# A table of steps ahead of which TensorE makes products of constants, and modulation rows one in each state step

## The reference

```python
def reference(x, ...):
    x = first_block(...)    # layer 0: gated linear attention (2 x 4 heads, chunks of 64) beside differential attention
                            # layer 1: state-space mixer (SSD, 32 heads in 4 groups, chunks of 128)
                            # each followed by layer norm, SwiGLU (hidden 2816), layer norm
    return second_block(...)  # SwiGLU; window attention beside a gated linear recurrence (HGRN); merge; SwiGLU

def first_block(...):         # per layer
    mod_x = silu(c) @ mod_w[layer] + mod_b[layer]          # modulation: six vectors of 1024
    mod_c = silu(c_ctx) @ mod_w[layer] + mod_b[layer]

def second_block(...):
    mod = silu(c) @ w_ada[l] + b_ada[l]                     # nine vectors of 1024
```

## Time and profile before

| | |
|---|---|
| median of 3 runs | 4111.59 us (4111.22 to 4112.58) |
| profiled execution | 4128.64 us |
| its span, first to last instruction | 4126.8 us |
| mean granted TensorE clock | 0.951 of 2.4 GHz |
| PE busy | 3827.0 us (93%) |
| DVE, ACT, POOL busy | 1596.6, 1431.0, 1181.7 us |

### The profile page before, as it was taken

The page is one execution under the profiler, slowest core; times in us unless marked ns, Lnnn a source line. Parts: engine busy times, 40 slices in busy tenths (PEclk is TensorE's granted clock), DMA queues, the critical chain, the costliest instruction groups (busy, mean ns, idle before and its releaser), DMA issues.

```text
span 4126.8 us, 52620 instructions
## 1 busy us (share of the span) xinstructions
PE 3827.0 (93%) x22147; PEld 3212.8 (78%) x22147; DVE 1596.6 (39%) x2686; ACT 1431.0 (35%) x2313; POOL 1181.7 (29%) x745
## 2 busy tenths in 40 slices
PE   7999889999998999998999899999988879898999
PEld 5877667888877888786888788888777766687888
DVE  4355563111136655655212321111457644332113
ACT  4223344211125434424422332211354536443223
POOL 2011022111132524516222421121433423243224
PEclk9999999999999999998999989999988989899999
DMA  5221133332241111023333412222322211142333
GB/s 177 72 78 42 47 113 108 97 97 91 93 141 37 42 52 50 28 65 125 98 103 105 139 58 67 62 62 64 115 71 62 57 43 32 43 146 82 97 97 108
DMA packets 471974, 336.67 MB, mean 82 GB/s; under 512 B 17609, under 2 KB 445627, under 8 KB 471739
## 3 DMA queue, kind: packets, MB, share of 16 engines
q1 hardware_dynamic: 471056, 333.05, 26.6%
q10 hardware_dynamic: 683, 0.26, 0.0%
HBM read 331.17 MB, written 2.10 MB: 81 GB/s over the span
## 4 chain that ended last, share of the span: by engine, by line
PE 81%; DVE 7%; ACT 4%; POOL 3%; DMA 2%; issue 2%; SPq 0%; ACTq 0%; POOLq 0%; DVEq 0%
PE PS L107 79%; PE PS L115 2%; DVE A L124 1%; POOL RWr L124 1%; DMA MW<-in_mod_w 1%; ACT A L118 1%; ACT L118 1%; POOL TM L124 1%; ACT RWH L121 1%; DVE A L132 1%; POOL A L124 1%; DMA MW<-in_w_ada 1%; DVE SM L144 1%; DVE XT L124 0%; DVE G L124 0%
## 5 line engine op out<-in xcount | busy, mean ns | idle before, releaser
L124 POOL TENSOR_TENSOR RWr<-RW,RWH 128x1024 fp32r<-128x1024 f32 (+2 forms) x316 | 727.9, 2306 | 2326.5 <-ACT RWH L121 2317.8
L107 PE MATMUL PS<-HTH,RWH 128*128 128x512 f32 (+1 forms) x3360 | 1211.1, 360 | 29.5 <-POOL RWr L124 9.2
L107 PE MATMUL PS<-HTr,RWH 128*128 128x512 f32 (+1 forms) x3360 | 1184.7, 353 | 0.0
L107 PE MATMUL PS<-HTH,RWr 128*128 128x512 f32 (+1 forms) x3360 | 1184.1, 352 | 0.0
L107 PE MATMUL PS<-Ar,RWH 128*128 128x512 f32 (+1 forms) x3264 | 825.6, 344 | 13.6 <-DVE XT L132 5.1
L107 PEld LDWEIGHTS PS<-HTH,RWH 128*128 128x128 f32 x3360 | 647.6, 193 | 146.3 <-issue 46.4
L107 PEld LDWEIGHTS PS<-HTH,RWr 128*128 128x128 f32 x3360 | 646.3, 192 | 85.6 <-issue 0.4
L107 PEld LDWEIGHTS PS<-HTr,RWH 128*128 128x128 f32 x3360 | 647.4, 193 | 82.0 <-issue 2.7
L107 PEld LDWEIGHTS PS<-Ar,RWH 128*128 128x128 f32 x3264 | 568.3, 193 | 102.5 <-issue 16.0
L121 ACT ACTIVATE RWH<-RW 128x1024 fp32r<-128x1024 f32 (+2 forms) x474 | 475.0, 1007 | 317.5 <-DMA RW<-in_ffn_w_out 163.6
L107 PE MATMUL PS<-Ar,RWr 128*128 128x512 f32 (+1 forms) x1632 | 555.5, 340 | 0.0
(11 more groups left out here) (193 smaller groups left out, 3790.7 us busy)
## 6 DMA issues: line engine op xcount, KB each, us to landing
RW<-in_ffn_w_in SPq DMA_DIRECT2D x176, 512.0 KB, 3.8
MW<-in_mod_w SPq DMA_DIRECT2D x83, 512.0 KB, 4.7
MW<-in_w_ada SPq DMA_DIRECT2D x72, 512.0 KB, 4.4
RW<-in_ffn_w_out SPq DMA_DIRECT2D x64, 512.0 KB, 3.9
RW<-in_ffn_w_out SPq DMA_DIRECT2D x64, 384.0 KB, 3.3
RW<-in_mix_w_in SPq DMA_DIRECT2D x41, 512.0 KB, 3.8
RW<-in_ssd_w_in SPq DMA_DIRECT2D x40, 512.0 KB, 3.9
RW<-in_ev_w_in SPq DMA_DIRECT2D x24, 512.0 KB, 3.9
```

The lines of the kernel that those rows point to most:

```text
L107: return self._ins(self.real and self.real.matmul(o, l, r, start=start, stop=stop, skip_group_check=True))
L124: return self._ins(self.real and self.real.tensor_tensor(out=o, in0=i0, in1=i1, op=op))
```

## The change

Two things. First, a table `warm` in `plan` names 71 steps by stage and arguments, each with a number from 2 to 11, 268 in sum. Ahead of such a step `tensor_program` calls `turn_over`, which asks `Banks.idle` for a PSUM bank that is free at that step, waits for that bank's last reader, and makes that many f32 products of `k.ident` with the first two matrices of `k.CC`, 256 columns, into it. Nobody reads them, and they signal nothing. If no bank is free nothing is made. Second, `Gla.states` puts `mod` after every state and not only the odd ones, and the two calls pass one row in place of two.

```diff
@@ class Banks
+    def idle(self, p, *key):
+
+        if p.real is None and key not in self.at:
+            at = [b for b in range(8) if 0 > self.back[b] or self.back[b] < self.step]
+            if not at:
+                return None
+            b = min(at, key=lambda b: self.back[b])
+            self.at[key], self.before[key] = (b, 1), [self.holder[b]] if self.holder[b] else []
+        if key not in self.at:
+            return None
+        for held in self.before[key]:
+            if p.real is not None:
+                for event in self.freed[held]:
+                    p.wait_ge(*event)
+        return self.of(*key)
+
...
+def turn_over(p, k, i):
+
+    pv = k.banks.idle(p, "warm", i)
+    if pv is not None:
+        for _ in range(k.warm[i]):
+            p.mm(pv[:, 0:256], k.ident, k.CC[:, 0:2, :].rearrange("p a b -> p (a b)"), True, True)
...
@@ class Gla
     def states(self, mod):
         out = []
         for x in range(11):
-            out += self.one(f"state {x}") + (mod if x % 2 else [])
+            out += self.one(f"state {x}") + mod
         return out
...
@@ def plan
-    order += gla[0].states([("mod", 24)] * 2) + spliced(gla[0].tail(), gla[1].early()) + [("mod_end", 24)]
+    order += gla[0].states([("mod", 24)]) + spliced(gla[0].tail(), gla[1].early()) + [("mod_end", 24)]
...
-    order += gla[1].states([("mod", 32)] * 2) + [("mark", "diff.start")]
+    order += gla[1].states([("mod", 32)]) + [("mark", "diff.start")]
...
-    steps = []
+    steps, warm = [], {
+        'Gla 0': {('q', 0): 4, ('v', 0): 3},
+        'MixOut m00': {('mix', 3, None): 3},
+        'Gla 1': {('fold', 3): 3},
+        'Diff': {('value', 3): 3, ('pc', 'v', 3, 0, 0): 3, ('value', 13): 9, ('wt', 20): 4, ('fold', 3, X): 3},
+        'Mod': {('row', 58): 6, ('turn', 11): 2, ('row', 107): 3, ('row', 111): 3, ('turn', 15): 2, ('row', 133): 3,
+            ('row', 142): 4, ('row', 147): 4, ('row', 166): 4},
+        'Head 0 ssd dt': {('tile', X, 0): 4},
+        'Head 0 f1 gate': {('tile', H0, 0): 10},
+        'Head 0 b2 gate': {('tile', H0, 0): 6},
+        'LayerNorm ssd': {('var', C, 0): 2},
+        'Ssd': {('z', 0, 0, 0): 2, ('z', 2, 0, 0): 2, ('z', 3, 0, 0): 2, ('ctr', 1, 5): 3, ('ctr', 2, 5): 3, ('ctr', 3,
+            5): 3, ('st', 0, 0, 0): 2, ('st', 1, 0, 0): 2, ('st', 2, 0, 0): 2, ('st', 3, 0, 0): 2, ('yd', 0, 0): 3,
+            ('yd', 2, 0): 3, ('yd', 3, 0): 3, ('yd', 0, 6): 3, ('yd', 1, 6): 3, ('yd', 2, 6): 3, ('yd', 3, 6): 3, ('yt',
+            3, 3): 2},
+        'Pre b1': {('var', H0, 0): 6, ('var', H1, 0): 6},
+        'LayerNorm e1': {('mean', H1): 4},
+        'Pre mix2': {('var', X, 1): 3, ('var', C, 0): 11},
+        'Hgrn': {('vt', 0): 4, ('l2', 0, 1, 3): 3, ('l2', 0, 1, 6): 5, ('l2', 1, 1, 6): 5, ('l2', 2, 1, 6): 5, ('l2', 1,
+            0, 0): 5, ('l2', 2, 0, 0): 5, ('l2', 3, 0, 0): 5, ('l2', 1, 1, 2): 5, ('l2', 2, 1, 3): 3, ('l2', 3, 0, 3):
+            4, ('l2', 3, 1, 1): 4, ('l2', 3, 1, 2): 3, ('l2', 3, 1, 3): 3, ('l2', 3, 1, 5): 2, ('l2', 3, 1, 6): 3},
+        'Window': {('rope', 1): 6, ('score', 0): 7, ('wt', 4): 3, ('wt', 23): 4, ('wt', 26): 3, ('wt', 27): 3, ('wt',
+            30): 4, ('wt', 31): 3},
+        'Merge': {('y', 0, H0): 2},
+        'Pre b2': {('var', H1, 0): 5},
+    }
...
+    k.warm = {i: warm[name(stage)][tuple(step)] for i, (stage, *step) in enumerate(steps)
+              if stage != "mark" and name(stage) in warm and tuple(step) in warm[name(stage)]}
     return steps
...
@@ def tensor_program
         elif (stage, *step) not in k.early:
+            if i in k.warm:
+                turn_over(p, k, i)
             stage.tensor(p, *step)
```

More of the change, by code:

```diff
@@ L197, with idle @@
 class AnyBank:
+    def idle(self, p, *key):
+        return self.of()
     def __init__(self, ps):
@@ L3517, in pads, with name @@
     return pad
+def name(stage):
+    if isinstance(stage, (Gla,)):
+        return f"Gla {stage.j}"
+    if isinstance(stage, (Pre, Post, LayerNorm, Modulate)):
+        return f"{type(stage).__name__} {stage.gen}"
+    if isinstance(stage, (MixOut, Ffn)):
+        return f"{type(stage).__name__} {stage.key}"
+    if isinstance(stage, Head):
+        return f"Head {stage.parts[0][0]} {stage.made[0].key[0]} {stage.made[0].key[1]}"
+    return type(stage).__name__
 def late_of_halves(k, gen):
```

## The result

| | before | after |
|---|---|---|
| median | 4112.09 us (4111.22 to 4127.22, 4 runs) | 4077.88 us (4066.20 to 4084.58, 4 runs) |
| profiled span | 4126.8 us | 4082.8 us |
| mean granted clock | 0.951 | 0.977 |

The ratio is 0.990, with a 95% interval of 0.9878 to 0.9923: 34 us less by the medians, 44 us less by the two profiled spans. Single executions of the changed kernel differ by 18 us, those of the kernel before by 16 us, so one pair of numbers says little here. The same kernel, timed again beside the kernel before (e9_again), gave 4072.71 us against 4117.65 us, 45 us less, ratio 0.9888 (0.9871 to 0.9905); 0.988 to 0.990 had been expected. The profiled execution of the changed kernel, 4084.58 us, was the slowest of its four. The forecast was 4060 us, in a range of 4036 to 4086 us.

What follows compares the result with a forecast made beforehand. The prediction took PE's own time as the bound, with about 404 us at 1.2 GHz. It summed −49 us for the products and −2 us for the rows, from 4111.6 us to 4060.6 us, range 4036 to 4086 us.

Steps and rivals of the forecast that it cites:

- What bounds the kernel: Whole kernel: PE's own time decides, busy 3827.0 of 4126.8 us, about 404 us of the span at 1.2 GHz.
- How much low time goes: At the 71 steps: 203 us less at 1.2 GHz, out of 338 us in 51 low stretches.
- The 0.6: Share of idle time ahead of the 71 steps that products cover, 115/193, taken also as the share of low time saved.
- What it is worth: Over the low stretches: 203 × 0.73 × 0.47 = 70 us, of which 0.7 is kept, 49 us; bounds 33 and 93 us.
- The pairs: Same work at both clocks, in the last big mixer and the linear recurrence: 0.47 and 0.46 us per us of low clock.
- What the products cost: 268 products at 0.43 us, 115 us at full clock, inside 193 us of waits: cost 0, upper bound 37 us.
- The bank wait: Ahead of each group, PE's wait for the last reader of the PSUM bank: cost 0, as banks were freed long ago.
- the slower rival: Ahead of the 71 steps: late bank readers delay products, slower from 1.8 us late on average, up to 4178 us; chance 0.03.
- one of the signs of being wrong: Ahead of the products: PE waiting for an ACT or DVE reader would show the forecast wrong.
- The rows: Modulation rows in the states of both heads: one after each of states 0 to 7; −2 us, bounds 0 and −5 us.
- The products don't count: At the 71 steps: the clock falls as before and the products lie in idle time, 4111 us; chance 0.05.
- More than I take: At the 71 steps: nearly every covered low stretch goes, 83 us gained, 4027 us; chance 0.08.

Runs made afterwards that it cites:

- e9_again, e9: The changed kernel, unaltered, timed again beside the kernel before; 4072.71 us against 4117.65 us, ratio 0.9888.
- e3: The changed kernel with one product of 8 columns in each of the 71 places; 4122.37 us, ratio 1.0005 to the kernel before.
- e4: The changed kernel with each product replaced by four transposes of a constant 128x128; 4070.84 us, ratio 0.9883 to the kernel before.
- e7: The changed kernel without three held groups, with more products in 19 old places and some new places, 335 in all; 4058.78 us, ratio 0.9849 to the kernel before.
- e11: As e7, with 31 products in 12 places more and 10 in four old ones, 376 in all; 4050.42 us, ratio 0.9833 to the kernel before.
- e1: The changed kernel's table of products alone, modulation rows left as in the kernel before; 4069.98 us, ratio 0.9884 to the kernel before.
- e5: The changed kernel without the three groups (10 products) ahead of which PE waited for a bank; 4072.89 us, ratio 0.9886 to the kernel before.
- e12: The changed kernel with 20 products in place of 3 at Diff value 3 and pc v 3; 4088.41 us, ratio 0.9930 to the kernel before.
- e2: The moved modulation rows alone, with the table of products emptied; 4124.10 us, ratio 1.0009 to the kernel before.
- e10: As e7, but with the modulation rows where they were in the kernel before; 4058.74 us, ratio 0.9855 to the kernel before.

## Why the prediction was right, point by point

**What bounds the kernel.** Right: the gain is PE's own work done at 2.4 GHz. e3 shows that it takes the work of the products, and e4 that their kind doesn't matter. Three readings in the text were off, and no term of the sum hangs on them: the page's clock row has eights in six slices, not seven; 14 of the 51 stretches lie between 1320 and 1922 us, not 18; and the 16 instructions of the earlier trace rows called transposes are eight f32 products of the state-space mixer with 128 columns (line 107, not 115).

**How much low time goes.** 203 us were forecast, 404.6 − 188.2 = 216 us went, and the mean clock is 0.977 (0.975 forecast). The 0.6 was a choice by the share of the waits that products fill; e7 and e11, which fill more, have less low time. Of the waits, 78 us stand behind the products in the changed kernel's trace, as the text worked out.

**What it is worth.** Mis-sized, twice, in opposite directions. I put 203 us of low time at 70 us of PE's work on the chain (203 × 0.73 × 0.47); PE's own work fell by 84.8 us, 0.39 us per us and not 0.34. And I kept 0.7 of it, giving back 21 us; the balance shows that 41 us were given back, and 0.52 kept (0.58 in the profiles of e9 and e1). 85 × 0.52 = 44 us against 49 us. That the two errors cancel is luck: with only the first put right the sum would have been 59 us, with only the second 36 us. The medians are 34 us apart in the first comparison and 45 us in the second, so the 49 us are near the measured gain, and how near can't be said. The pairs hold: yd 0 to yd 6 of group 0 takes 30.36 us at a clock of 1.00, and the part of the recurrence at head 0 takes 4.09 us, as head 2 did:

```profile
1367.25:1397.61 30.36, 27.90 (x203) 23.45 (x203) 23.80 (x44) 21.15 (x49) 27.52 (x25) 1.00 0.00 1
...
3075.08:3079.17 4.09, 4.09 (x34) 4.09 (x35) 3.24 (x6) 0.63 (x1) 1.29 (x1) 1.00 0.00 0
```

33.15 − 30.36 = 2.8 us for 6.6 us of low time is 0.42, a little under the 0.47.

**What the products cost.** 0 holds as far as the runs can tell: 134.2 us busy, 0.50 us each with the pipeline tail, nearly all within the waits, and taking out the 10 late ones changed nothing that can be measured (e5). What the late ones cost is a part of the 41 us given back. The fit of the products is seen at yd 0, where 2.40 us of wait became:

```profile
1364.68 1.46 PE L107 MATMUL PS<-CC 128*128 128x256 f32 x6
1367.25 2.00 PE L107 MATMUL PS<-TM,G 128*128 128x64 f32 x16 [1.10 <-DVE G L124]
```

**The bank wait.** I costed it at 0 because the banks had been free for long, and named it as the slower rival. It exists, in three of 71 places, so one of the signs of being wrong that the prediction named came true there. In these places the argument failed: the order of the list says nothing of how far ACT is behind. Its price with 2 to 4 products a place is too small to measure (e5), and with 20 in two of them it is 15.7 us more (e12), the full price. The rival needed 1.8 us of lateness in the mean place; most places show no wait ahead of the products, 4.5 us in all.

**The rows.** Wrong. Their DMA waits shrink from 10.9 to 7.4 us as the step said, and PE is up to 6.5 us ahead, but the −2 us isn't there: e2 is at 1.0009. The step carried the gain past the differential attention without asking what an earlier PE meets there. It waits 1.06 us longer for ACT at pc v 1, and the clock falls behind waits where it had not fallen before, 13.7 us of low time in four stretches of e2. These falls are there in the kernels with the table and the moved rows as well, and e10, with the old rows, is level with e7: the rows can be left out.

**The other rivals.** "The products don't count" is refuted by e1, e3 and e4. "More than I take" describes e11, not the change: 67 us less than before, with 376 products.

What stays open: how the 41 us given back divide into waits for DVE, POOL and ACT that begin earlier, and products that came late; what each place at the norms brings; and why the moved rows bring falls of the clock in the differential attention.

## What to carry to other kernels

Where TensorE sets the time and its granted clock falls behind short waits, products that nobody reads can hold the clock up at no cost, as long as they end before the wait does. At Window score 0, 13 products of 0.43 us filled a wait of 6.4 us down to 0.6 us; as an estimate from this place, a wait of w us takes about (w − 0.6)/0.43 products of this size. Read from the next trace what is left over. Put them only where the bank that they write is read in time, which the timeline shows as a wait behind the products and not ahead of them. Before counting a gain in one stage, look at what the engine waits for in the next, and whether its clock falls there: a lead of 6.5 us was gone there. Compare stages over several traces: one profile hid what the norms bring.

## What the runs showed of the hardware

f32 transposes against the identity kept TensorE at 2.4 GHz as products did (e4 and e1: mean clock 0.981 and 0.982, 133.7 and 133.6 us busy). Over a whole kernel a us at the lower level that was saved made PE's own work 0.39 us shorter (84.8 us for 216 us; 0.41 in e1). Executions of one kernel on one core spread by half a per cent: the kernel before had 4107.6 to 4130.7 us in 23 executions, and the two profiled executions of the changed kernel had 188.2 and 170.6 us of low clock. The falls don't come at the same waits in every execution: one profile has low stretches at 299 and 323 us, the other has none from 253 to 365 us. So the gain of a single place can't be read from one profile.
